# The experts' down biases taken out of the steps and added per token tile, and one VectorE operation moved ahead of another

## The reference

```python
logits = t @ w_router + b_router
top_val, top_idx = top_k(logits, 4);  gate = softmax(top_val)
# tokens are sorted by expert and cut into chunks of up to 128 slots; for each chunk of expert e:
gu = xc @ w_gate_up[e] + b_gate_up[e]          # 1024 -> 2048
g, u = min(gu[:, :1024], 7), clip(gu[:, 1024:], -7, 7)
act = (u + 1) * (g * sigmoid(1.702 * g))
y = act @ w_down[e] + b_down[e]                 # 1024 -> 1024
out[token] += y * gate_of_slot
```

## Time and profile before

| what | value |
|---|---|
| runs | median 2043.04 us of 3 (2042.1 to 2043.36) |
| profiled execution | 2039.13 us, its span 2037.5 us |
| mean granted TensorE clock | 0.983 |
| busy: PE / DVE / ACT / POOL | 1953.8 / 1564.4 / 1280.0 / 291.9 us |
| moved by DMA | 489.99 MB, mean 240 GB/s |

### The profile page before, as it was taken

One profiled execution on the slowest core, in us unless ns is written; L12 is line 12 of the kernel. 1 busy time (PEld: TensorE's weight loads), 2 busy tenths in 40 slices (PEclk: granted clock), 3 DMA queues, 4 the chain that ended last, 5 costly groups with the idle time before them and its releaser, 6 DMA issues.

```text
span 2037.5 us, 36966 instructions
## 1 busy us (share of the span) xinstructions
PE 1953.8 (96%) x11706; PEld 1520.2 (75%) x11707; DVE 1564.4 (77%) x2025; ACT 1280.0 (63%) x1772; POOL 291.9 (14%) x350
## 2 busy tenths in 40 slices
PE   7999999999996999999999999999999999999993
PEld 6777778888685777777777778877778877777783
DVE  4788855566657879788777779977879988976896
ACT  5555555454534767667666568756667767755775
POOL 3100000000135211102211110211111101211110
PEclk8999999999997999999999999999999999999997
DMA  5030111011445978989887799979889989888995
GB/s 185 21 104 1 41 43 42 21 42 42 155 189 171 331 264 298 373 296 371 290 281 270 268 362 374 334 268 358 298 291 374 379 289 370 314 276 292 377 372 194
DMA packets 256288, 489.99 MB, mean 240 GB/s; under 512 B 20194, under 2 KB 38478, under 8 KB 256144
## 3 DMA queue, kind: packets, MB, share of 16 engines
q1 hardware_dynamic: 233824, 439.56, 59.8%
q0 software_dynamic: 21376, 49.81, 9.0%
q10 hardware_dynamic: 1040, 0.00, 0.0%
HBM read 461.66 MB, written 32.18 MB: 242 GB/s over the span
## 4 chain that ended last, share of the span: by engine, by line
PE 88%; DVE 5%; issue 2%; ACT 2%; DMA 1%; POOL 1%; POOLq 0%; ACTq 0%; SPq 0%; DVEq 0%
PE psum L836 17%; PE psum L837 17%; PE psum L840 17%; PE psum L849 8%; PE psum L513 3%; PE psum L515 3%; PE psum L514 3%; PE psum L646 3%; PE psum L650 3%; PE psum L648 3%; PE psum L822 3%; PE psum L796 1%; PE psum L866 1%; PE psum L769 1%; PE psum L770 1%
## 5 line engine op out<-in xcount | busy, mean ns | idle before, releaser
L1917 DVE TENSOR_TENSOR w_lo<-ring,w_hi 128x1024 fp32r<-128x1024 f32 x768 | 908.8, 1221 | 98.0 <-ACT w_hi L1197 87.1
L1197 ACT ACTIVATE w_hi<-ring 128x1024 fp32r<-128x1024 f32 x768 | 789.6, 1058 | 126.1 <-PE psum L840 120.0
L836 PE MATMUL psum<-w_hi,rows_hi 128*128 128x512 f32 x1024 | 425.9, 416 | 0.0
L837 PE MATMUL psum<-w_hi,rows_lo 128*128 128x512 f32 x1024 | 400.3, 391 | 0.0
L840 PE MATMUL psum<-w_lo,rows_hi 128*128 128x512 f32 x1024 | 316.3, 390 | 0.0
L840 PEld LDWEIGHTS psum<-w_lo,rows_hi 128*128 128x128 f32 x1024 | 192.8, 188 | 41.4
L837 PEld LDWEIGHTS psum<-w_hi,rows_lo 128*128 128x128 f32 x1024 | 193.4, 189 | 38.2
L836 PEld LDWEIGHTS psum<-w_hi,rows_hi 128*128 128x128 f32 x1024 | 194.0, 189 | 36.6
L836 PE MATMUL psum<-w_hi,act_hi 128*128 128x512 f32 x512 | 215.2, 420 | 0.0
L837 PE MATMUL psum<-w_hi,act_lo 128*128 128x512 f32 x512 | 199.8, 390 | 0.5 <-issue 0.5
L849 PE MATMUL psum<-ring,region_m 128*32 128x256 f32 x3072 | 171.9, 379 | 0.0
(11 more groups left out here) (373 smaller groups left out, 3009.4 us busy)
## 6 DMA issues: line engine op xcount, KB each, us to landing
ring<-in_w_gate_up_dram SPq DMA_DIRECT2D x128, 2048.0 KB, 17.8
ring<-in_w_down_dram SPq DMA_DIRECT2D x64, 2048.0 KB, 12.8
ring<-in_w_in_dram SPq DMA_DIRECT2D x16, 512.0 KB, 5.1
region_m<-in_x_dram SPq DMA_DIRECT2D x8, 512.0 KB, 9.4
ring<-in_w_in_dram SPq DMA_DIRECT2D x2, 2048.0 KB, 15.7
ring<-in_w_out_dram SPq DMA_DIRECT2D x2, 2048.0 KB, 7.8
region_a<-in_x_dram POOLq DMA_DIRECT2D x8, 512.0 KB, 5.2
acc_rows<-region_a POOLq DMA_DIRECT2D x8, 512.0 KB, 3.7
```

What stands on the lines that cost most here:

```text
L836: mm(bank(i), hi[:, ks], wh, start=False, stop=False)
L837: mm(bank(i), lo[:, ks], wh, start=False, stop=False)
L1197: act.activation(w_hi[:, n % NBUF, :], place[i][:, k0 * HALF:(k0 + 2) * HALF], ACT.Copy).then_inc(hi_done, 1)
L1917: v.tensor_tensor(out=w_lo[:, n % NBUF, :], in0=place[i][:, k0 * HALF:(k0 + 2) * HALF], in1=w_hi[:, n % NBUF, :].bitcast(f32), op=ALU.subt ...
```

## The change

The down bias leaves the steps: the sums of units 4 and 5 start with the first product (`start=True` there), and the tail's four narrow down biases go. `bias3` holds only the gate and up biases.

In its place each token tile gets its share: ScalarE takes the exponential of all 32 logits (`share_exp`), VectorE multiplies by the reciprocal of the gates' sum and the mask of the four chosen experts, three times side by side (`share_rows`); TensorE turns the 96 columns; ScalarE copies them and VectorE makes the middle 32 rows the low part (`share_low`); TensorE multiplies by the down biases (`share_w`: high, high, low; two matmuls of 512 columns, `share_mm`); ScalarE copies the 1024 columns out to SBUF; and POOL adds the 128 rows to `acc_rows` with an accumulating indirect DMA (`share_add`). One semaphore, `share_step`, counts seven steps per tile. Tiles 0 to 3 go through this in the router stage, during tiles 4 to 7, by one set of buffers (`share_g`, `share_gT`, `share_out[0]`); tiles 4 to 7 go through it in the hand-over, in two pairs, by buffers of their own. These buffers lie in the ring slots of `w_hi` and `w_lo` and in the place of the second output row buffer, so ScalarE's third high piece of the first step, VectorE's fourth low piece and ScalarE's first output of the second step wait for them. POOL's requests for the first step's successor (`next_rows`) move ahead of the loop, the four late adds stand behind them, and a load of 256 columns of the final gain stands behind the adds.

Apart from that, VectorE's `actT_low(0)` moves from behind the low half of piece 16 to behind that of piece 15. The small sums for the first rows move from PSUM bank 5 to bank 0.

The core of the diff:

```diff
@@ PE: router stage, tile t @@
+            def share_mm(dst, turned, signal=True):
+                for half in range(2):
+                    last = mm(dst[:, half * HALF:(half + 1) * HALF], turned, share_w[0:3 * NE, half * HALF:(half + 1) * HALF],
+                              start=True, stop=True)
+                if signal:
+                    last.then_inc(share_step, 1)
...
                         for k in range(KD):
+                            if half == 1 and k == 6 and t >= 4:
+                                pe.wait_ge(share_step, 7 * (t - 4) + 2)
+                                tr(bank(7)[0:3 * NE, 2 * P:3 * P], share_g.rearrange("p w e -> p (w e)"), ident[:]).then_inc(share_step, 1)
...
                     router_sum(t - 2)
+                if 4 <= t < NT:
+                    pe.wait_ge(share_step, 7 * (t - 4) + 5)
+                    share_mm(bank(4, 2), share_gT[0:3 * NE, :])
+                    pe.wait_ge(share_step, 7 * (t - 3))
                 if 1 <= t <= NT:
                     router_T(t - 1)
@@ PE: hand-over @@
+            pe.wait_ge(share_step, SHARE_LAST + 2)
+            for q in range(4):
+                last = tr(bank(3)[0:3 * NE, q * P:(q + 1) * P], share_g4[:, q].rearrange("p w e -> p (w e)"), ident[:])
+            last.then_inc(share_step, 1)
+            pe.wait_ge(share_step, SHARE_LAST + 5)
+            share_mm(bank(4, 2), share_gT4[0:3 * NE, 0, :], signal=False)
+            share_mm(bank(2, 2), share_gT4[0:3 * NE, 1, :])
             pe.wait_ge(first_built, 3)
...
             rows_turn()
+            pe.wait_ge(share_step, SHARE_LAST + 7)
+            share_mm(bank(4, 2), share_gT4[0:3 * NE, 2, :], signal=False)
+            share_mm(bank(2, 2), share_gT4[0:3 * NE, 3, :])
@@ PE: loop @@
-                        if k0 == 0:
+                        if k0 == 0 and i < 4:
                             bias(bank(i), i, 0, HALF, P)
...
-                            mm(bank(i), hi[:, ks], wh, start=False, stop=False)
+                            mm(bank(i), hi[:, ks], wh, start=(i >= 4 and k0 + q == 0), stop=False)
...
-                                tail_bias(bank(1)[:, QC:2 * QC], (4, 5))
@@ ACT: router stage, tile t @@
                     part_out(t - 2)
+                if t >= 4:
+                    act.wait_ge(share_step, 7 * (t - 4) + 3)
+                    act.activation(share_gT[0:3 * NE, :], bank(7)[0:3 * NE, 2 * P:3 * P], ACT.Copy).then_inc(share_step, 1)
+                    act.wait_ge(share_step, 7 * (t - 4) + 6)
+                    if t >= 5:
+                        act.wait_ge(share_added, 16 * (t - 4))
+                    act.activation(share_out[0], bank(4, 2), ACT.Copy).then_inc(share_step, 1)
                 act.wait_ge(x2_done, t + 1)
...
                     gate_exp(t - 3)
+                    share_exp(t - 3).then_inc(share_step, 1)
@@ ACT: hand-over @@
             for n in range(NBUF):
+                if n == 2:
+                    act.wait_ge(share_added, 16 * (NT - 4))
                 high(n, 0)
+            act.wait_ge(share_step, SHARE_LAST + 3)
+            act.activation(share_gT4[0:3 * NE], bank(3)[0:3 * NE, :].rearrange("p (t s) -> p t s", t=4), ACT.Copy).then_inc(share_step, 1)
+            act.wait_ge(share_step, SHARE_LAST + 6)
+            act.activation(share_out[1], bank(4, 2), ACT.Copy)
+            act.activation(share_out[2], bank(2, 2), ACT.Copy).then_inc(share_step, 1)
             act.wait_ge(rowsT_mm, 1)
             rowsT_out()
+            act.wait_ge(share_step, SHARE_LAST + 8)
+            act.activation(share_out[3], bank(4, 2), ACT.Copy)
+            act.activation(share_out[4], bank(2, 2), ACT.Copy).then_inc(share_step, 1)
@@ POOL @@
+            def share_add(t, src):
+                g.indirect_dma_start(out=acc_rows, out_offset=bass.IndirectOffsetOnAxis(ap=entry[:, t, 0, 0:1], axis=0),
+                                     in_=src, in_offset=None, bounds_check=SEQ - 1, oob_is_err=False,
+                                     compute_op=ALU.add).then_inc(share_added, 16)
...
                 if 3 <= t < NT - 1:
                     scatter(t - 3)
+                if t >= 4:
+                    pool.wait_ge(share_step, 7 * (t - 3))
+                    share_add(t - 4, share_out[0])
...
+            next_rows(0, 0, tail, before, e_next, c_next, t_next)
+            pool.wait_ge(share_step, SHARE_LAST + 9)
+            for t in range(NT - 4, NT):
+                share_add(t, share_out[t - NT + 5])
+            pool.wait_ge(share_added, 16 * NT)
@@ DVE @@
+            def share_rows(t, dst):
+                return v.scalar_tensor_tensor(out=dst, in0=bc(logit[:, t, None, :], [P, 3, NE]), scalar=gsum[:, t:t + 1],
+                                              in1=bc(mask_b[:, t, None, :], [P, 3, NE]), op0=ALU.mult, op1=ALU.mult)
...
             for t in range(NT):
+                if t >= 4:
+                    dve.wait_ge(share_step, 7 * (t - 4) + 4)
+                    share_low(share_gT[NE:2 * NE, :], bank(7)[NE:2 * NE, 2 * P:3 * P]).then_inc(share_step, 1)
                 dve.wait_ge(wo_mm, t + 1)
...
                     place_rows(t - 3)
+                    dve.wait_ge(share_step, 7 * (t - 3) + 1)
+                    share_rows(t - 3, share_g).then_inc(share_step, 1)
@@ DVE: loop @@
-                                    if n == 16:
+                                    if n == 15:
                                         actT_low(0)
```

More of the change, by code:

```diff
@@ L849, in tail_product @@
                                 last = mm(dst[TAIL * q:TAIL * (q + 1), :], stat_of(k), wu[i][:, k, c:c + QC],
-                                          start=False, stop=(k == KD - 1))
+                                          start=(not biased and k == 0), stop=(k == KD - 1))
                         return last
@@ L1150, in gate_exp, with share_exp @@
                 act.activation(gate4[:, t, :], gate4[:, t, :], ACT.Exp, accum_out=gsum[:, t:t + 1]).then_inc(gexp_done, 1)
+            def share_exp(t):
+                act.wait_ge(mask_done, t + 1)
+                return act.activation(logit[:, t, :], logit[:, t, :], ACT.Exp, bias=top_neg[:, t:t + 1])
             for q in range(4):
@@ L1182, in _ @@
             gate_exp(NT - 1)
+            for t in range(NT - 4, NT):
+                last = share_exp(t)
+            last.then_inc(share_step, 1)
             act.wait_ge(bias_done, 2)
-            act.activation(bias3[64:96, :], bstage[64:96, :], ACT.Copy).then_inc(bias_done, 1)
+            act.activation(bias3[64:96, :], bstage[64:96, 0:2 * D], ACT.Copy).then_inc(bias_done, 1)
             act.wait_ge(bias_done, 3)
@@ L1240, in output @@
                                 def output(half):
+                                    if u == 1 and half == 0:
+                                        act.wait_ge(share_added, 16 * NT)
                                     act.wait_ge(sub_mm, unit_end(4 + half, j))
@@ L1439, in _, with next_rows @@
             pool.nop()
+            def next_rows(u, j, tail, before, e_next, c_next, t_next):
+                g.dma_start(meta[:, 1 - u, :], chunks[ds(e_next * (SEQ // P) + c_next, 1)].rearrange("a s w -> (a s) w")).then_inc(meta_in, 16)
+                with pool.If(t_next > 0):
+                    tail_rows(1 - u, e_next, c_next)
+                wait_reg(pool, meta_in, j * 16 + 16)
+                wait_reg(pool, rowsT_mm, j + 1)
+                gather(1 - u)
+                with pool.If(t_next > 0):
+                    with pool.If(tail > 0):
+                        wait_reg(pool, trowsT_mm, before + 1)
+                    tail_gather(1 - u, before + tail)
+                pool.nop()
+            pool.wait_ge(added, 32)
+            pool.wait_ge(tadded, 16)
+            _, _, tail, before, _, t_next, _ = load_step(pool, 0)
+            e_next, c_next, _, _, _, _, _ = load_step(pool, 1)
+            next_rows(0, 0, tail, before, e_next, c_next, t_next)
+            pool.wait_ge(share_step, SHARE_LAST + 9)
+            for t in range(NT - 4, NT):
+                share_add(t, share_out[t - NT + 5])
+            pool.wait_ge(share_added, 16 * NT)
+            pool.wait_ge(first_built, 3)
+            g.dma_start(gfin[:, HALF:3 * QC], norm_final_g[None, HALF:3 * QC].to_broadcast([P, QC])).then_inc(norm_in, 16)
             with pool.Fori(0, MAXS // GROUP_STEPS) as group:
@@ L1911, in _ @@
             v.scalar_tensor_tensor(out=word_c, in0=short_c, scalar=256.0, in1=word_c, op0=ALU.mult, op1=ALU.add).then_inc(columns_done, 1)
+            for t in range(NT - 2, NT):
+                gate_rden(t)
+            dve.wait_ge(share_step, SHARE_LAST + 1)
+            for t in range(NT - 4, NT):
+                last = share_rows(t, share_g4[:, t - (NT - 4)])
+            last.then_inc(share_step, 1)
             def low(n, j):
@@ L1945, in _ @@
             dve.wait_ge(count_mm, 3)
-            v.tensor_reduce(out=meta[:, 0, 1:2].bitcast(f32), in_=bank(5)[:, 2:5], axis=AX, op=ALU.add).then_inc(first_meta, 1)
```

(3 more changed lines are left out.)

75 lines of the change are left out of this document (45 added, 30 removed).

## The result

Before 2042.57 us (median of 4 runs, 2040.26 to 2043.36), after 2061.94 us (4 runs, 2060.78 to 2063.18): ratio 1.0097, 95% interval 1.0085 to 1.011. The change costs 19.4 us. The forecast was 2050, so the sign held and the size did not: +6.7 was forecast. The range (2037 to 2062) held by 0.06 us, and by luck: no rival of the prediction has the 10.2 us between router stage and loop that make most of the difference.

The account below looks back on a forecast made before the run. TensorE was taken to bound the kernel (88% of the chain of waits). Loop -20.6, router stage +26.8 and hand-over +0.5 gave +6.7 us, carried to the median 2043.04: 2049.7, say 2050 us; range 2037 to 2062.

Parts of the forecast that it names:

- The router stage: Tiles 4 to 7: each ScalarE copy waits for the previous tile's add to land; 26.8 us more.
- L: Router stage: landing time of a share's accumulating DMA after its issue, taken as 6.0 us, ends 2.9 and 10.2.
- Net +0.5, between 0 and 2.5: Between router stage and loop: first step starts about 2.4 us later, mostly offset by a gather issued a little sooner.
- the adds of the fourth share beside the first weights: Before the first step: together with ScalarE's copies for the first pair, they put its start back about 2.4 us.
- its lost saving: First step: its own saving of 0.64 us is swallowed by the gather of the next rows.
- The late adds: Four adds on POOL behind the next rows' gather: delay the third step's gather to near 726 us, hidden, 4 in hand.
- The loop: Expert loop: biases removed and activations' low half moved give 21.2 us less, 20.6 after the first step's loss.
- 0.645: Step without a tail: 0.46 us from two wide biases plus 0.185 of stall removed by the move; 10.3 us over 16.
- 0.68: Step with a tail: 0.46 us from wide biases plus 0.22 from narrow ones; 10.9 us over 16.
- the loop gives back less: Rival: VectorE or full queues keep steps without a tail at 36 us, total 2060; chance 0.10.
- The ring doesn't hold: Rival, router stage: previous add already landed at ScalarE's copy, only TensorE's 1.7 us a tile paid, total 2029; chance 0.14.
- the ring: Router stage: copy, square, second norm, top and slots, four scatters, add, next copy; periods 22.2, 22.6, 21.1 us.

Follow-up runs that it names:

- all loop edits: The kernel before with the loop part of the change alone (wide and narrow down biases gone, activations' low half moved), no share computed: 2024.54 us, ratio 0.9917.
- move: The kernel before with only the first activations' low half at piece 15 instead of 16 on VectorE: 2038.47 us, ratio 0.9987.
- narrow: The kernel before without the four narrow down biases of a tail, all else as before: 2039.88 us, ratio 0.9990.
- wide: The kernel before without the two wide down biases of a step, all else as before: 2036.64 us, ratio 0.9961.
- 39 fillers: The kernel before with 39 more instructions at TensorE's start that only raise a semaphore: 2048.31 us, ratio 1.0034.
- branch: The kernel before with a never-taken branch of 200 filling instructions at TensorE's start: ratio 1.0012.
- early add: The changed kernel with POOL issuing the router stage's share adds right behind the write of the residual, ahead of the four scatters: 2038.73 us, ratio 0.9988 to before.
- no late adds: The changed kernel without the adds of the last four shares and ScalarE's later wait for their landing: 2061.44 us, ratio 1.0098 to before.
- after with the branch: The changed kernel whole, with 200 filling instructions in a never-taken branch at TensorE's start: 2061.49 us, ratio 1.0077 to before.

## Why the prediction was right or wrong

**The router stage: right, in mechanism and size.** Forecast +26.8, measured +27.06. The periods 23.1, 22.4, 20.8 stand against 22.2, 22.6, 21.1. The adds take 7.3, 6.65 and 6.1 us from issue to landing in the chain; L was 6.0. One aside on the way to L is not shown: that a plain write moves half as much as the add. The add's packets count 0.50 MB, the plain write 512 KB. With the add moved the 27.1 become 5.6.

**Hand-over and first step: the step that failed.** "Net +0.5, between 0 and 2.5" was 10.2 in the traces. Two pieces were missing.
- The fourth share's add. I counted its copies and "the adds of the fourth share beside the first weights" at 2.4 gross. From the square of tile 7 to the first bias it is 33.2 us in after. In the kernels with the hand-over of before it is 27.6 to 30.1 (before, all loop edits, move, narrow, wide, 39 fillers, branch), 28.7 in the mean; before's own 27.56 is the lowest of them, so some 1.1 of the 5.7 is chance. With the early add, the fourth one done before the weights are asked for, it is 30.1, and the weights take 10.0 us instead of 15.2. So that add costs about 3.1, and products and copies about 1.4: 4.5, not 2.4 for both.
- The first step. I costed it at nothing beyond its lost saving, because a gather ended it anyway. The pause of 4.2 us, with the clock at half speed for 5.8 us behind it, comes from the place of the code and is worth 7.4 us in the trace (39.04 to 31.65 with the branch). That before's step was only 4.6 shorter than after's is in part chance: in the ten kernels without a long pause the step takes 30.4 to 37.4 us, and in the two longest TensorE waits for weights (2.5 and 3.5 us). No row that I gave showed it; the 0.49 us "issue" behind the same jump in before was in the trace, and I did not ask what it would become if the program moved. The late adds, which I had put off as hidden, were nearly so: leaving them out moves the time by 0.5 us, inside the measurement.

**The loop: mechanism right, the tail's price wrong.** -20.6 forecast, -13.7 measured. A step without a tail gives 0.60 of 0.645. With a tail it gives 0.37 of 0.68: 16 x (0.045 + 0.31) = 5.7 us short. The four narrow biases and the wide one held back the second matmul by 0.68 us; I took that difference as what would go. In after the same place reads:

```profile
1113.71 0.50 PE L869 MATMUL psum<-w_hi,act_hi 128*128 128x512 f32 x1
1114.05 0.40 PE L870 MATMUL psum<-w_hi,act_lo 128*128 128x512 f32 x1
```

Now the first full matmul behind the tail's narrow products holds back the second by 0.34 instead of the dense 0.23. Part of the price belonged to the change from narrow to full and stayed: 0.11 there, and another 0.11 because the first full matmul starts later behind the narrow ones (11.68 us after the turns of the tail's rows, 1102.03 to 1113.71; in before the first narrow bias starts 11.57 us after them, 1068.11 to 1079.68). The last 0.1 of the 0.31 can't be placed in one wait. Another 1.0 us is one late step. POOL's timeline and TensorE's turns of the step that took 36.49:

```profile
1593.85 5.20 POOL L1562 DMA_INDIRECT acc_rows<-region_m,meta  x1 [20.86 <-ACT region_m L1301]
1609.06 0.60 POOL L1507 DMA_DIRECT2D meta<-slot_tab  x1 [10.01 <-issue]
1614.91 1.10 POOL L1476 DMA_INDIRECT region_m<-h_rows,meta  x1 [5.26 <-DMA meta<-slot_tab]
```

```profile
1622.16 1.06 PE L819 MATMUL psum<-ident,region_m 128*128 128x128 f32 x8 [0.85 <-DMA region_m<-h_rows,meta]
```

A y add that takes 5.2 us to issue stands ahead of the late gather. Of the eight kernels with all of the loop's edits five lose about 1.0 us so, in one step each, behind y adds of 4.1 to 5.3 us, and three in none. Not every long y add has this effect: in the kernel without late adds four of over 5 us make no step late.

**The sum again, with what was measured:** 27.1 + 5.7 + 4.6 - 13.7 = 23.7 in the traces, 19.4 in the medians. The rival "the loop gives back less" named the right place and the wrong cause: VectorE and the transfers do not hold steps without a tail at 36 us. "The ring doesn't hold" described, at 2029, the kernel with the early add but for the hand-over, the first step and the tails: 2038.7.

## What to carry to other kernels

When one buffer is refilled behind a DMA, follow the ring all the way round the other engines' queues: where the issue stands in a program decides more than how long the transfer takes (27 us became 5.6 by moving one issue). Price two edits at one wait together and not by themselves, and do not take the difference between two patterns as the price of the instructions in it. Where control flow jumps over code that has not run yet, adding instructions anywhere earlier can put the arrival of later ones on the critical path; test it with instructions that do nothing before looking for a cause in the new work.

## What the runs showed of the hardware

- 39 instructions that do nothing cost 6.2 us (0.21 to 0.48% of the time), mostly by one pause of 4.24 us behind a jump and the lower clock behind it (granted clock 0.67 up to the turns).
- Such a wait ends 1.4 to 1.6 us after a packet of 0.02 MB on the instruction queue q8 has landed, in six kernels. The loop shows it on its first pass alone: after it one such packet comes in 1321 us.
- Beside the fourth share's add the first weights are there 14.1 to 15.5 us after the request (after, no late adds, after with the branch), without it 9.9 to 10.5 (four kernels).
- A semaphore increment that runs costs TensorE about 0.11 us; a branch over 200 of them at the start costs 2.1 us (ratio 1.0003 to 1.0021), though TensorE waits for VectorE there.
- An accumulating DMA of 512 KB lands 6.1 to 7.3 us after its issue in the quiet router stage, against 8.5 to 10.2 in the steps.
- POOL needs up to 5.27 us to issue a y add in after, against 2.54 at most in before; the kernel with the loop edits alone shows 5.28 too, so the shares are not the cause, and with the move, the narrow or the wide biases alone it is 2.69 at most. Why is not settled.
